# Second output group of a two-layer trunk in seven products, its fourth token sum in another buffer, large transfers in pieces

## The chip, the cores and the metric

The kernel runs on one core of one Trainium2 chip. The metric is the device time of one execution in microseconds; less is better. The engines are named as the profile names them: PE is TensorE's matmul, PEld its weight load, DVE is VectorE, ACT is ScalarE, POOL is GpSimd, SP is SyncE, which here only issues transfers.

## What is computed

Two layers over 1024 tokens of 2048 features, all in float32. Each layer is one large input projection (2048 to 4352), a small middle part, and one large output projection (2048 to 2048) that is added to x:

```python
for l in range(DEPTH):                                    # DEPTH = 2
    h = _rmsnorm(x, norm_gain[l])
    proj = jnp.einsum('bsd,de->bse', h, w_in[l])
    q, k, v, g_attn, x_rnn, g_rnn = jnp.split(proj, splits, axis=-1)
    attn = _swa_sink_attention(q, k, v, sinks[l], cos, sin)
    xc = _causal_conv(x_rnn, conv_w[l], conv_b[l])
    rnn = _rg_lru(xc, w_rgate[l], b_rgate[l], w_igate[l], b_igate[l], lru_param[l])
    mixed = jnp.concatenate([attn * jax.nn.silu(g_attn), rnn * jax.nn.silu(g_rnn)], axis=-1)
    x = x + jnp.einsum('bse,ed->bsd', mixed, w_out[l])
return _rmsnorm(x, final_gain)
```

`_rg_lru` has two gate matrices of 64x64 blocks on the convolved `xc`, then a scan over tokens.

## The kernel before

**Passes, groups, units.** The tokens are taken in two halves `h` of 512, the layers `l` in order, so there are four passes (h, l): (0,0), (0,1), (1,0), (1,1). In a pass the columns of both projections are cut into 25 groups of 256: groups 0 to 16 are the input projection, 17 to 24 the output projection (`PG = 17`). A plain group is 8 units; a unit is one 256 KB weight load and 12 matmuls of 512 tokens (three for each 128x128 block, since weights and operands are cut into a high and a low part, L719). Time inside a pass is counted in slots `s`, eight to a group; each engine's program runs through the same slots, in a fixed order within a slot, and engines meet only at semaphores.

**Seven products.** Groups in `SEVEN` (L68) take half of their inner dimension by a Strassen scheme over two halves of the features, the tokens and the columns: instead of four of the eight units they have seven units of 12 matmuls of 256 tokens (L740), four of them ("lead") in the slots of the group before. They need four weight sums S1 to S4, made ahead of time in DRAM, and four pairs of token sums. Before, these are the output groups 19 to 24 in every pass (23 as the last in (1,1)), and in (1,0) and (1,1) the input groups 7 to 15 too.

**Token sums of the output side.** `operand_sums` (four DVE instructions, L1381 to L1384) builds the raw sums of pair n in slot `T_AT[n]`; one slot later ACT cuts the high part (`xsum_cut_hi`, L950) and DVE the low part (`operand_sums_lo`, L1390). `T_ORDER` says which pair comes n-th. The buffers lie over storage that is free by then: pairs 0 and 1 over the end of `q`, 2 and 3 over the recurrent half of `mixed`, so that 2 and 3 wait until those tiles are cut.

**Weights.** SP issues the load of unit u+6 when unit u is done (`RING = 6`). In the slot of unit u, ACT cuts the high part of unit u+3 (`weight_hi`, L942) and DVE the low part (`weight_lo`, L1344; `AHEAD = 3`). From then on PE can run it.

**The recurrent tiles.** Eight tiles j start at slots `R0`. For the last, j = 7, that is slot 112: DVE does the convolution taps in slots 113 and 114 (L1604, L1607, L1609), cuts its low part into `xcut` in slot 116 (`conv_lo`, L1621), and PE runs the gate matmuls on it at the end of slot 117 (`gate`, L867), which wait for that cut (`xc_lo`) and stand in PE's one stream with everything else.

**Weight sums.** POOL makes them with transfers from DRAM to DRAM (copies L631, accumulating ones L637), in batches of up to two groups. `OPENS` holds the batches at which POOL waits for a later unit, so the batches run in stretches: 5, 6, 2 and 3 before.

**Other large transfers.** In (1,1) SP spills x in four transfers of 1 MB (slots 1 to 4); in (1,0) it stores the first half's output in four of 1 MB (slots 22, 30, 38, 46); in (0,1) it loads the next half's x in two bursts (slots 148 and 196). Where they stand in SP's queue they stand before the next weight load.

Of the kernel before, what the change touches and what calls it, by code (L numbers as in the profile page):

```python
# [13 lines left out]
P = 128  # L14
DEPTH = 2
D = 2048
SEQ = 1024
TOK = 512
# [49 lines left out]
SEVEN = {(h, l): (*IN_SEVEN[h, l], *range(PG + 2, PG + (7 if (h, l) == (LAST, DEPTH - 1) else 8)))  # L68
# [121 lines left out]
def tile_of(what, t):  # L190

    return 2 * GROUPS.index((what, t // 2)) + t % 2
# [35 lines left out]
OPENS = {5: (0, 1, 1), 11: (1, 0, 4), 13: (1, 1, 8)}  # L228
# [16 lines left out]
def build(nc, xt, w, blocks, gates, par, fgain, cossin, ident, out):  # L245
    with ExitStack() as ctx:
        def sb(name, shape, dt=F32):
            return ctx.enter_context(nc.sbuf_tensor(name, [P, *shape], dt))
# [23 lines left out]
        gt = sb("gt", [TOK])  # L272
        prob = sb("prob", [2, 2, 2, P])
# [23 lines left out]
        idn = probT[:, 0, 0, 0, :]  # L297
# [4 lines left out]
        t_at = {"out": [(q_end if i < 2 else mixed_end) - (2 - i % 2) * t_size for i in range(NPAIR)]}  # L302
# [190 lines left out]
        def _(sp_):  # L493
# [36 lines left out]
            for h in range(HALVES):  # L530
                for l in range(DEPTH):
                    for s in range(SLOTS):
# [18 lines left out]
                        if (h, l, "in") in ZONES and l == 1 and s - SPILL_AT in range(4):  # L551
                            i = SPILL[s - SPILL_AT]

                            sp_.wait_ge(evac, at_evac(h, 0, tile_of("o", 4 * i + 3)))
                            sp_.dma_start(x_kept[i], x[:, 4 * i:4 * i + 4, :].rearrange("p k t -> p (k t)")
                                          ).then_inc(kept[i], 16)
                        for i in range(KT // 2):
                            if (h, l) in X_BACK and s == RELOAD + 2 * i:

                                if (h, l, "in") in ZONES:  # L560
                                    sp_.wait_ge(unit_done, TURNED[h, l, "in"])
                                if l == 0:
                                    if h > 0:
                                        sp_.wait_ge(stored[i // 2], 16 * h)
                                    sp_.dma_start(x[:, 2 * i:2 * i + 2, :], xt[h, :, 2 * i:2 * i + 2, :]
                                                  ).then_inc(xres_in[i], 16)
                                else:
                                    sp_.wait_ge(kept[i // 2], 16 * sum(at < (h, l) for at in X_BACK if at[1] == 1) + 16)
                                    half = i % 2 * 2 * TOK
                                    sp_.dma_start(x[:, 2 * i:2 * i + 2, :].rearrange("p k t -> p (k t)"),  # L570
                                                  x_kept[i // 2, :, half:half + 2 * TOK]).then_inc(xres_in[i], 16)
                        for a, b in STORES_W:
                            if h > 0 and l == 0 and s == NS + 2 * b:

                                sp_.wait_ge(scaled, (h - 1) * KT + b)
                                sp_.dma_start(out[h - 1, :, a:b, :], x[:, a:b, :]).then_inc(stored[a // 4], 16)
# [6 lines left out]
                        if l == 1 and s == O0 + 12 and h == LAST:  # L583

                            sp_.wait_ge(v_done, per_layer(h, l, NP, NP))
                            sp_.dma_start(idn, ident).then_inc(idn_in, 16)
                        if l == 1 and s == O0 + 12 and h < LAST:

                            sp_.wait_ge(op_lo, at_op(h, 1, 1, KT - 1))
                            sp_.wait_ge(xsum_done, at_t(h, 1, "out", NPAIR - 1))  # L590
                            for i in range(KT // 4):
                                x_load(h + 1, i)
                        if l == 1 and s == O0 + (OG - 1) * UPG + 4 and h < LAST:

                            sp_.wait_ge(unit_done, TURNED[h, 1, "out"])
                            for i in range(KT // 4, KT // 2):
                                x_load(h + 1, i)
# [17 lines left out]
            for n in stored:  # L615
                sp_.wait_ge(n, 16 * LAST)
# [54 lines left out]
        def _(pe):  # L671
# [233 lines left out]
            def fin_transposes(n):  # L905
# [13 lines left out]
                for k in range(4):  # L919
                    t0 = HT + P * c  # L920
                    last = pe.transpose(fin_bank(n)[:, P * k:P * k + P], x[:, 4 * g + k, t0:t0 + P], idn[:, :])
# [14 lines left out]
        def _(act):  # L936
# [7 lines left out]
            def xsum_cut_hi(h, l, zone, n):  # L944
# [3 lines left out]
                if zone == "out" and i >= 2:  # L948
                    act.wait_ge(op_lo, at_op(h, l, 1, AT + RT // 2 * (i - 1) - 1))
# [373 lines left out]
        def _(dve):  # L1323
# [23 lines left out]
            def operand_sums(h, l, zone, n):  # L1347
# [6 lines left out]
                if zone == "in":  # L1354
# [3 lines left out]
                    if l == 1:  # L1358
                        dve.wait_ge(kept[T_ROOM[i]], 16 * sum(at <= (h, l) for at in X_BACK if at[1] == 1))
                        dve.wait_ge(op_lo, at_op(h, l, 0, KT - 1))  # L1360
                        dve.wait_ge(acc_done, at_acc(h, KT * 2))
                    else:
                        for k in (pair, pair + 1):
                            dve.wait_ge(x_sem(k), 16 * (h + 1))
                        if h > 0:
                            dve.wait_ge(stored[T_ROOM[i]], 16 * h)
# [12 lines left out]
                if i >= 2:  # L1379
                    dve.wait_ge(op_lo, at_op(h, l, 1, AT + RT // 2 * (i - 1) - 1))  # L1380
# [544 lines left out]
```

## Time and profile before

| | us |
|---|---|
| median of 3 runs | 2288.71 |
| lowest and highest | 2285.85, 2288.94 |
| the profiled execution's own time | 2291.39 |
| its span | 2289.6 |

| engine | busy us | share of the span |
|---|---|---|
| PE | 2278.3 | 100% |
| PEld | 1940.8 | 85% |
| DVE | 1567.5 | 68% |
| ACT | 1313.7 | 57% |
| POOL | 84.7 | 4% |

The mean granted clock of TensorE over the span is 0.999 of full speed. PE is never long idle, so what an edit is worth is read from PE's own rows (how far one matmul starts after the other, where a gap stands) and from the other engines' rows in the slots where PE waits for them. A shift of any other engine's work costs only what reaches PE.

### The profile page before, as it was taken

To read this page: it belongs to the slowest core of one execution; us is meant where nothing else is said; L and a number is where in the kernel's file an instruction comes from. 1 tells how busy PE (TensorE), PEld (TensorE's weight loads), DVE (VectorE), ACT (ScalarE), POOL (GpSimd) and SP (SyncE) were. 2 spreads that over 40 slices of the span, in tenths; PEclk is the share of its full clock that TensorE was granted. 3 is DMA by queue.
4 is the path that set the end of the run, shared out by engine and by line. 5 is a ranking of instruction groups with operands and counts; after the bars stand their busy time and mean duration, and the time that the engine had idled before them with its cause. 6 is when DMAs were issued, how large, how long until landed. Compare 5 with 4: busy or idle time off the path is not lost.

```text
span 2289.6 us, 38210 instructions
## 1 busy us (share of the span) xinstructions
PE 2278.3 (100%) x14446; PEld 1940.8 (85%) x14446; DVE 1567.5 (68%) x2594; ACT 1313.7 (57%) x2536; POOL 84.7 (4%) x138
## 2 busy tenths in 40 slices
PE   9999999999999999999999999999999999999998
PEld 7878888899888888889987888888988888888898
DVE  7658878656546876856677777686568468778555
ACT  6558666444445867645665576663446557566444
POOL 0110000000111000000010000000001100000000
PEclk9999999999999999999999999999999999999999
DMA  8988777544788877644476466664447746666444
GB/s 246 240 247 264 240 243 237 157 134 143 198 243 235 261 236 239 213 142 139 138 231 182 158 206 195 219 190 147 139 134 255 194 134 198 205 201 199 139 134 152
DMA packets 173271, 447.01 MB, mean 195 GB/s; under 512 B 20768, under 2 KB 25120, under 8 KB 167200
## 3 DMA queue, kind: packets, MB, share of 16 engines
q1 hardware_dynamic: 165744, 381.56, 52.3%
q0 software_dynamic: 6912, 62.92, 11.6%
q8 instruction: 114, 1.87, 0.3%
q14 instruction: 69, 0.57, 0.1%
q10 hardware_dynamic: 432, 0.10, 0.0%
HBM read 365.85 MB, written 141.56 MB: 222 GB/s over the span
## 4 chain that ended last, share of the span: by engine, by line
PE 95%; DMA 2%; DVE 2%; ACT 1%; issue 0%; POOL 0%; DVEq 0%; ACTq 0%; POOLq 0%
PE proj L719 71%; PE proj L740 18%; DMA wall<-in_w 2%; PE ps_at L848 2%; PE ps_at L823 1%; PE ps_at L867 1%; PE proj L759 1%; DMA wall<-in_blocks 0%; DVE wcut L1344 0%; ACT wcut L942 0%; ACT gy L1048 0%; PE proj L786 0%; PE ps_at L674 0%; DVE mixed L1828 0%; DVE rstd L1457 0%
## 5 line engine op out<-in xcount | busy, mean ns | idle before, releaser
L719 PE MATMUL proj<-operand,wcut 128*128 128x512 f32 x7512 | 1747.9, 391 | 3.5 <-DVE gy L1476 2.2
L719 PEld LDWEIGHTS proj<-operand,wcut 128*128 128x128 f32 x7512 | 1400.9, 188 | 302.6 <-issue 8.6
L1344 DVE TENSOR_TENSOR wcut<-wall,wcut 128x512 fp32r<-128x512 f32 x799 | 549.9, 688 | 548.0 <-ACT wcut L942 541.2
L942 ACT ACTIVATE wcut<-wall 128x512 fp32r<-128x512 f32 x798 | 501.7, 629 | 605.2 <-DMA wall<-in_w 326.4
L740 PEld LDWEIGHTS proj<-operand,wcut 128*128 128x128 f32 x1476 | 187.8, 191 | 6.5
L740 PE MATMUL proj<-operand,wcut 128*128 128x256 f32 x1476 | 189.8, 283 | 0.0
L740 PE MATMUL proj<-xsum_out,wcut 128*128 128x256 f32 x1104 | 136.8, 283 | 0.0
L740 PEld LDWEIGHTS proj<-xsum_out,wcut 128*128 128x128 f32 x1104 | 134.9, 192 | 0.6
L740 PE MATMUL proj<-xsum_in,wcut 128*128 128x256 f32 x864 | 111.8, 284 | 0.0
L740 PEld LDWEIGHTS proj<-xsum_in,wcut 128*128 128x128 f32 x864 | 107.9, 191 | 3.5 <-issue 1.7
L1048 ACT ACTIVATE gy<-proj 32x512 f32<-32x512 f32 x144 | 85.0, 590 | 15.5 <-PE proj L719 8.7
L1100 ACT ACTIVATE prob<-ps_at,stat 128x128 f32<-128x128 f32 x256 | 90.3, 367 | 0.7
L1139 ACT ACTIVATE sqr<-ps_at,pars 64x512 f32<-64x512 f32 x64 | 43.8, 685 | 59.0 <-PE ps_at L867 58.5
L1113 ACT ACTIVATE mixed<-ps_at 64x256 f32<-64x256 f32 x128 | 48.6, 380 | 42.6 <-PE ps_at L848 38.6
L1005 ACT ACTIVATE sqr<-x 128x512 f32<-128x512 f32 x62 | 37.0, 635 | 55.9 <-DVE x L1654 55.9
L1654 DVE TENSOR_TENSOR x<-proj,x 128x512 f32<-128x512 f32 x62 | 39.9, 686 | 39.7 <-PE proj L719 39.6
L631 POOL DMA_DIRECT2D weight_sums<-in_blocks x32 | 16.1, 511 | 1353.3 <-PE proj L719 1353.1
L1439 DVE TENSOR_TENSOR acc<-acc,sqr 128x512 f32<-128x512 f32 x80 | 55.2, 690 | 4.9 <-ACT sqr L1005 0.2
L637 POOL DMA_DIRECT2D weight_sums<-in_blocks x64 | 51.0, 861 | 178.9 <-DMA weight_sums<-weight_sums 97.1
L1100 ACT ACTIVATION_READ_ACCUMULATOR prob<-ps_at,stat 128x1 f32 x256 | 52.8, 206 | 0.0
L1539 DVE TENSOR_TENSOR gy<-proj,rstd 128x512 f32<-128x512 f32 x56 | 38.5, 687 | 18.9 <-PE proj L719 18.3
L1607 DVE SCALAR_TENSOR_TENSOR xc<-xr,pars,xc 128x512 f32<-128x512 f32 x64 | 47.9, 749 | 1.4
(186 smaller groups left out, 1734.2 us busy)
## 6 DMA issues: line engine op xcount, KB each, us to landing
wall<-in_w SPq DMA_DIRECT2D x494, 256.0 KB, 2.8
weight_cuts<-wcut SPq DMA_DIRECT2D x126, 512.0 KB, 4.0
wcut<-weight_cuts SPq DMA_DIRECT2D x126, 512.0 KB, 4.1
weight_sums<-in_blocks POOLq DMA_DIRECT2D x84, 512.0 KB, 6.5
wall<-weight_sums SPq DMA_DIRECT2D x164, 256.0 KB, 2.7
wall<-in_blocks SPq DMA_DIRECT2D x141, 256.0 KB, 2.8
weight_sums<-weight_sums POOLq DMA_DIRECT2D x28, 512.0 KB, 5.0
x<-in_xt SPq DMA_DIRECT2D x16, 512.0 KB, 3.7
```

What stands on the lines that cost most here:

```text
L637: pool.dma_start(sums[SUMS[to], l, g:g + size].rearrange("g r e -> (g r) e"), blocks[WHOLE[what], l, g:g + size].rearrange("g r e -> (g r) ...
L719: last = pe.matmul(bank_of(l, 2 * g + m)[:, :], wcut[:, n % RING, a, c:c + P], operand[:, k, b, :], start=(i == 0 and k == 0), stop=(k == ...
L740: last = pe.matmul(bank_of(l, 2 * g + m)[:, HT * half:HT * half + HT], wcut[:, n % RING, a, P * i:P * i + P], src, start=(kind == "lead" a ...
L848: last = pe.matmul(ps_v[HD * i:HD * i + HD, t, :, :], vkey[kv][rows, 2 * c + b, :], probT[rows, :, i, :, SB * b:SB * b + SB], start=b == 0 ...
L942: act.activation(wcut[:, u % RING, 0, :], wall[:, u % RING, 1, :], ACT.Copy).then_inc(w_hi, 1)
L1048: act.activation(gy[dst:dst + 32, 1, :], bank_of(l, tile)[src:src + 32, :], ACT.Copy).then_inc(shift_done, 1)
L1100: act.activation(prob[:, odd, i, pair, :], ps_s[:, odd, i, pair, :], ACT.Exp, scale=HD ** -0.5, bias=stat[:, 1, odd, i, pair:pair + 1], ac ...
L1113: act.activation(mixed[HD * odd:HD * odd + HD, TPK * kv:TPK * kv + TPK, t0:t0 + CH], ps_v[HD * i:HD * i + HD, :, odd, :], ACT.Copy).then_i ...
L1139: act.activation(r_in[a:a + HD, :], ps_at[a:a + HD, 3, :], ACT.Tanh, scale=0.5, bias=pars[a:a + HD, l, C_BR + j:C_BR + j + 1]).then_inc(r_ ...
L1344: dve.tensor_tensor(wcut[:, u % RING, 1, :], wall[:, u % RING, 1, :], wcut[:, u % RING, 0, :].bitcast(F32), ALU.subtract).then_inc(w_lo, 1)
L1439: ins = dve.tensor_tensor(acc[:, :], acc[:, :], sqr[:, k % 2, :], ALU.add)
L1607: mark(dve.scalar_tensor_tensor(xc[:, :], src, wc, xc[:, :], ALU.mult, ALU.add))
```

## The change

1. Group 18, the second output group, is done in seven products too, in all four passes.
2. Its leads stand in the slots of group 17, so the token sums are made earlier: slots 113, 115, 127 and 135 in place of 126, 128, 136 and 143. The third to be made is now pair 3, and its buffer lies over `prob` and `probT`, the attention probabilities; the identity that was kept in `probT` goes to `kboth`.
3. Weight sums for group 18 are added, so there are 18 batches in place of 16, in stretches of 5, 5, 1, 2, 1 and 4. The two stretches of one batch start at slot 128 of (0,1) and of (1,0).
4. The spill goes in eight transfers of 512 KB (slots 1 to 8), the output store in sixteen of 256 KB (every second slot from 16 to 46), the loads of the next half's x one by one in slots 148, 152, 156, 160 and 196 to 199.

```diff
-SEVEN = {(h, l): (*IN_SEVEN[h, l], *range(PG + 2, PG + (7 if (h, l) == (LAST, DEPTH - 1) else 8)))
+SEVEN = {(h, l): (*IN_SEVEN[h, l], *range(PG + 1, PG + (7 if (h, l) == (LAST, DEPTH - 1) else 8)))
...
-T_AT = {(h, l, "out"): (126, 128, 136, 143) for h in range(HALVES) for l in range(DEPTH)}
+T_AT = {(h, l, "out"): (113, 115, 127, 135) for h in range(HALVES) for l in range(DEPTH)}
...
-T_ORDER = {(h, l, "out"): (0, 1, 2, 3) for h in range(HALVES) for l in range(DEPTH)}
+T_ORDER = {(h, l, "out"): (0, 1, 3, 2) for h in range(HALVES) for l in range(DEPTH)}
...
-OPENS = {5: (0, 1, 1), 11: (1, 0, 4), 13: (1, 1, 8)}
+OPENS = {5: (0, 1, 1), 10: (0, 1, 128), 11: (1, 0, 4), 13: (1, 0, 128), 14: (1, 1, 9)}
...
-        t_at = {"out": [(q_end if i < 2 else mixed_end) - (2 - i % 2) * t_size for i in range(NPAIR)]}
+        t_at = {"out": [q_end - 2 * t_size, q_end - t_size, mixed_end - 2 * t_size, prob_at]}
...
-                        if (h, l, "in") in ZONES and l == 1 and s - SPILL_AT in range(4):
+                        if (h, l, "in") in ZONES and l == 1 and s - SPILL_AT in range(8):
...
-                        for a, b in STORES_W:
-                            if h > 0 and l == 0 and s == NS + 2 * b:
+                        for k in range(KT):
+                            if h > 0 and l == 0 and s == NS + 2 * k + 2:
...
-                if i >= 2:
-                    dve.wait_ge(op_lo, at_op(h, l, 1, AT + RT // 2 * (i - 1) - 1))
+                if i == 2:
+                    dve.wait_ge(op_lo, at_op(h, l, 1, AT + RT // 2 - 1))
+                if i == 3:
+                    dve.wait_ge(pt_done, per_layer(h, l, NP, NP))
```

The instructions of DVE in slots 115 and 116 of pass (0,0), up to the cut that the gate of tile 7 waits for (`xcut`). Lines above 620 are two to four higher in the changed kernel. Before:

```order
L1344 TENSOR_TENSOR wcut<-wall,wcut 128x512
L1637 SCALAR_TENSOR_TENSOR mu<-sqr,mu 128x512
L1614 TENSOR_TENSOR gwcut<-gw,gwcut 128x2x128
L1344 TENSOR_TENSOR wcut<-wall,wcut 128x512
L1621 TENSOR_TENSOR xcut<-xc,xcut 64x512 x2
```

And in the changed kernel:

```order
L1346 TENSOR_TENSOR wcut<-wall,wcut 128x512
L1385 TENSOR_TENSOR xraw_out_59<-mixed 128x256
L1386 TENSOR_TENSOR xraw_out_59<-mixed,xraw_out_59 128x256
L1387 TENSOR_TENSOR xraw_out_59<-mixed 128x256
L1388 TENSOR_TENSOR xraw_out_59<-mixed,xraw_out_59 128x256
L1641 SCALAR_TENSOR_TENSOR mu<-sqr,mu 128x512
L1618 TENSOR_TENSOR gwcut<-gw,gwcut 128x2x128
L1346 TENSOR_TENSOR wcut<-wall,wcut 128x512
L1394 TENSOR_TENSOR xsum_out_51<-xraw_out_59,xsum_out_51 128x1024
L1625 TENSOR_TENSOR xcut<-xc,xcut 64x512 x2
```

The sums of pair 1 and the cut of their low part now stand ahead of the cut for the gate. Those of pair 0 (xraw_out_58 and xsum_out_50) stand likewise in slots 113 and 114, just ahead of these rows.

PE in pass (0,0), from the last gate matmul of tile 7 to the first two leads. Before:

```order
L867 MATMUL ps_at<-xcut,gwcut 128x512 x2
L719 MATMUL proj<-operand,wcut 128x512 x348
L740 MATMUL proj<-operand,wcut 128x256 x12
L719 MATMUL proj<-operand,wcut 128x512 x12
L740 MATMUL proj<-xsum_out_50,wcut 128x256 x3
```

And in the changed kernel:

```order
L869 MATMUL ps_at<-xcut,gwcut 128x512 x2
L721 MATMUL proj<-operand,wcut 128x512 x252
L742 MATMUL proj<-operand,wcut 128x256 x12
L721 MATMUL proj<-operand,wcut 128x512 x12
L742 MATMUL proj<-xsum_out_50,wcut 128x256 x3
```

The first lead comes 96 matmuls, which is one plain group, earlier, and the pattern that follows it is one group longer.

## Rows read from the trace of the kernel before

**Rows 1.** The page, part 1: busy time, share, instructions of each engine.
```profile
PE 2278.3 (100%) x14446; PEld 1940.8 (85%) x14446; DVE 1567.5 (68%) x2594; ACT 1313.7 (57%) x2536; POOL 84.7 (4%) x138
```

**Rows 2.** The chain in order of time: start us, us, what; pass (0,0).
```profile
365.29 78.92 PE proj L719 x348
...
482.04 8.19 PE proj L719 x36
...
503.04 8.19 PE proj L719 x36
```

**Rows 3.** Timeline (start us, us, instruction, [idle before]) of (0,0), slots 113 to 119.
```profile
344.69 0.69 DVE L1344 TENSOR_TENSOR wcut<-wall,wcut 128x512 fp32r<-128x512 f32 x1 [1.84 <-ACT wcut L942]
...
354.40 1.40 DVE L1621 TENSOR_TENSOR xcut<-xc,xcut 64x512 fp32r<-64x512 f32 x2
...
358.72 0.62 PE L867 MATMUL ps_at<-xcut,gwcut 128*128 128x512 f32 x2
...
362.87 1.42 DVE L1344 TENSOR_TENSOR wcut<-wall,wcut 128x512 fp32r<-128x512 f32 x2 [2.17 <-ACT wcut L942]
```

**Rows 4.** Timeline of DVE where the token sums stand before, slots 126 to 128.
```profile
386.18 0.42 DVE L1381 TENSOR_TENSOR xraw_out<-mixed 128x256 f32<-128x256 f32 x1
...
387.90 0.68 DVE L1539 TENSOR_TENSOR gy<-proj,rstd 128x512 f32<-128x512 f32 x1
...
954.80 1.23 DVE L1390 TENSOR_TENSOR xsum_out<-xraw_out,xsum_out 128x1024 fp32r<-128x1024 f32 x1 [0.47 <-ACT xsum_out L950]
955.98 0.69 DVE L1344 TENSOR_TENSOR wcut<-wall,wcut 128x512 fp32r<-128x512 f32 x1
```

**Rows 5.** Who waited for L1621 (us, times), and the timeline of (0,1).
```profile
  PEld ps_at L867: 0.8, 2
...
925.13 1.40 DVE L1621 TENSOR_TENSOR xcut<-xc,xcut 64x512 fp32r<-64x512 f32 x2
...
929.45 0.62 PE L867 MATMUL ps_at<-xcut,gwcut 128*128 128x512 f32 x2
```

**Rows 6.** Timeline of (1,0), slots 114 to 117; last, the high cut.
```profile
1491.64 0.63 ACT L942 ACTIVATE wcut<-wall 128x512 fp32r<-128x512 f32 x1 [3.30 <-DMA wall<-weight_sums]
1492.38 0.69 DVE L1344 TENSOR_TENSOR wcut<-wall,wcut 128x512 fp32r<-128x512 f32 x1 [2.60 <-ACT wcut L942]
1493.10 0.75 DVE L1607 SCALAR_TENSOR_TENSOR xc<-xr,pars,xc 128x512 f32<-128x512 f32 x1
...
1498.87 1.41 DVE L1621 TENSOR_TENSOR xcut<-xc,xcut 64x512 fp32r<-64x512 f32 x2
...
1502.90 0.63 PE L867 MATMUL ps_at<-xcut,gwcut 128*128 128x512 f32 x2
...
1522.58 1.06 ACT L950 ACTIVATE xsum_out<-xraw_out 128x1024 fp32r<-128x1024 f32 x1 [3.67 <-DVE xraw_out L1384]
```

**Rows 7.** Timeline of (1,1), slots 114 to 117.
```profile
2052.34 0.63 ACT L942 ACTIVATE wcut<-wall 128x512 fp32r<-128x512 f32 x1 [2.38 <-DMA wall<-weight_sums]
...
2053.80 0.75 DVE L1607 SCALAR_TENSOR_TENSOR xc<-xr,pars,xc 128x512 f32<-128x512 f32 x1
...
2059.57 1.40 DVE L1621 TENSOR_TENSOR xcut<-xc,xcut 64x512 fp32r<-64x512 f32 x2
...
2064.51 0.63 PE L867 MATMUL ps_at<-xcut,gwcut 128*128 128x512 f32 x2
```

**Rows 8.** Around 1215 us: chain, PE's timeline, windows (stretch, busy times, PEclk, DMA).
```profile
1199.27 10.87 DMA wall<-in_w
...
1217.14 5.04 PE L719 MATMUL proj<-operand,wcut 128*128 128x512 f32 x14 [1.81 <-DVE gy L1476]
...
1217.40:1220.90 3.50, 3.50 (x10) 2.68 (x10) 3.34 (x7) 3.37 (x6) 0.00 (x0) 0.52 0.96 255
```

**Rows 9.** POOL's timeline there, and the page's weight loads (count, KB, us to landing).
```profile
1197.64 1.60 POOL L637 DMA_DIRECT2D weight_sums<-in_blocks  x2 [0.61 <-DMA weight_sums<-in_blocks]
...
wall<-in_w SPq DMA_DIRECT2D x494, 256.0 KB, 2.8
```

More of the change, by code:

```diff
@@ L272, in build @@
         gt = sb("gt", [TOK])
+        prob_at = nc.sbuf_base
         prob = sb("prob", [2, 2, 2, P])
@@ L567, in _ @@
                                 else:
-                                    sp_.wait_ge(kept[i // 2], 16 * sum(at < (h, l) for at in X_BACK if at[1] == 1) + 16)
+                                    sp_.wait_ge(kept[i // 2], 32 * sum(at < (h, l) for at in X_BACK if at[1] == 1) + 32)
                                     half = i % 2 * 2 * TOK
@@ L583, in _ @@
                         if l == 1 and s == O0 + 12 and h == LAST:
-                            sp_.wait_ge(v_done, per_layer(h, l, NP, NP))
+                            sp_.wait_ge(s_done, per_layer(h, l, NP, NP) + 1)
                             sp_.dma_start(idn, ident).then_inc(idn_in, 16)
[L587 to L591, printed above, removed]
+                        for i in range(KT // 4):
+                            if l == 1 and s == O0 + 12 + 4 * i and h < LAST:
+                                if i == 0:
+                                    sp_.wait_ge(op_lo, at_op(h, 1, 1, KT - 1))
+                                    sp_.wait_ge(xsum_done, at_t(h, 1, "out", NPAIR - 1))
                                 x_load(h + 1, i)
-                        if l == 1 and s == O0 + (OG - 1) * UPG + 4 and h < LAST:
-                            sp_.wait_ge(unit_done, TURNED[h, 1, "out"])
-                            for i in range(KT // 4, KT // 2):
+                        for i in range(KT // 4, KT // 2):
+                            if l == 1 and s == O0 + (OG - 1) * UPG + i and h < LAST:
+                                sp_.wait_ge(unit_done, TURNED[h, 1, "out"])
                                 x_load(h + 1, i)
@@ L615, in _ @@
             for n in stored:
[L616 removed]
+                sp_.wait_ge(n, 64 * LAST)
         @block.gpsimd
@@ L920, in fin_transposes @@
                     t0 = HT + P * c
-                    last = pe.transpose(fin_bank(n)[:, P * k:P * k + P], x[:, 4 * g + k, t0:t0 + P], idn[:, :])
+                    last = pe.transpose(fin_bank(n)[:, P * k:P * k + P], x[:, 4 * g + k, t0:t0 + P], idn)
                 last.then_inc(fin_t, 1)
@@ L947, in xsum_cut_hi @@
                 act.wait_ge(xsum_done, at_t(h, l, zone, n))
-                if zone == "out" and i >= 2:
-                    act.wait_ge(op_lo, at_op(h, l, 1, AT + RT // 2 * (i - 1) - 1))
+                if zone == "out" and i == 2:
+                    act.wait_ge(op_lo, at_op(h, l, 1, AT + RT // 2 - 1))
                 act.activation(xsum[zone][i][:, HI_PART[zone][i], :, :], xraw[zone][i][:, :, :],
@@ L1358, in operand_sums @@
                     if l == 1:
-                        dve.wait_ge(kept[T_ROOM[i]], 16 * sum(at <= (h, l) for at in X_BACK if at[1] == 1))
+                        dve.wait_ge(kept[T_ROOM[i]], 32 * sum(at <= (h, l) for at in X_BACK if at[1] == 1))
                         dve.wait_ge(op_lo, at_op(h, l, 0, KT - 1))
```

17 lines of the change are left out of this document (9 added, 8 removed).

## The prediction

> **What bounds the kernel now.** I read the page first. PE is busy for 2278.3 of 2289.6 us [rows 1], so there are two ways to change the time: change how long PE's own stream is, or change how long PE stands still in it. I then read the chain in order of time for the price of a group [rows 2], the timelines of DVE and PE at the slots into which work is moved [rows 3 to 7], and the largest standstill of PE that the trace has [rows 8, 9]. The reader is to see that DVE, busy 68% of the span on average, has no free time in the few slots that matter.
>
> The profiled execution took 2291.39 us, 2.7 above the median of 2288.71. I make the sum against 2291.4 and take the 2.7 off at the end.
>
> **Group 18 in seven products.** 348 plain matmuls take 78.92 us, so one starts 0.2268 us after the other, and a plain group of 96 takes 21.77 us [rows 2]. A group in the seven-product pattern repeats after 503.04 - 482.04 = 21.00 us [rows 2]; that holds 48 matmuls of 512 and 84 of 256 tokens. The pattern moves one group forward and becomes one group longer, so each pass saves 0.77 us, four passes **3.1 us**. It is all on PE, so all of it is on the path. The three additional weight units of each pass and the lead copies fall into slots 137 to 151. Nothing of that is new in kind: the groups behind it run the same work at the 21.00 us period without PE waiting. The pair sums that stood in slots 126 to 129 and at 143 leave this region, so DVE is less late there than before. I cost it at nothing; if a weight cut came late, it would cost its delay, some tenths.
>
> **The first two token sums, moved to slots 113 and 115.** This is the term that decides. The four raw sums of a pair take 387.90 - 386.18 = 1.72 us of DVE from the first to the next instruction, the low cut 955.98 - 954.80 = 1.18 us [rows 4], so a pair costs 2.90 us and two pairs 5.80 us. All of it now stands ahead of L1621, the cut on which the gate matmuls of tile 7 wait. DVE and ACT run their instructions in program order, so L1621 moves by what is put ahead of it, less the idle time that DVE has in between.
>
> Pass (0,0): DVE waits before the weight cut at 344.69 and not again until 362.87 [rows 3]. The sums stand behind the cut at 344.69, so nothing of the wait before it hides them. L1621 ends at 354.40 + 1.40 = 355.80; the gate starts at 358.72. The cover is 2.92 us, the shift 5.80, so PE stands still for **2.9 us**. I followed ACT through the same slots: its high cut of a pair takes 1.06 us [rows 6] and is ready before DVE comes to the low cut, so it adds nothing.
>
> Pass (0,1): L1621 ends at 926.53, the gate starts at 929.45 [rows 5]. The cover is again 2.92, the standstill **2.9 us**.
>
> Pass (1,0): here the raw sums of pair 0 fit into the 2.60 us in which DVE waits for a weight cut [rows 6]. ACT's cut of them can start behind its weight cut, at 1491.64 + 0.63 = 1492.27, and ends about 1493.35. DVE's low cut then ends about 1494.55, where L1607 started at 1493.10 before: a shift of 1.45. The sums of pair 1 and their low cut add 2.90, 4.35 in all. The cover is 1502.90 - 1500.28 = 2.62 [rows 6], the standstill **1.7 us**, some of it at the unit before the gate, whose weight cut is late as well.
>
> Pass (1,1): the same shape, with ACT's weight cut ending at 2052.97 and L1607 at 2053.80 [rows 7], so again a shift of 4.35. The cover is 2064.51 - 2060.97 = 3.54, the standstill **0.8 us**.
>
> Together 8.3 us. That PE does wait at this place is in the trace: tile 5 of (0,0) and of (0,1) has next to no cover and PE waited twice there, 0.8 us in all [rows 5]. The ends: 0, if I overlook cover; 11.2, if DVE's idle time in (1,0) and (1,1) hid nothing (5.80 - 2.62 and 5.80 - 3.54 in place of 1.7 and 0.8). A gain is excluded, since nothing is taken from DVE ahead of L1621. I take 8.3, as every part of it is a difference of two rows. Behind the standstill PE's other suppliers have that much more time, so nothing else is late next.
>
> **What a standstill does to the clock.** When PE had been idle for 1.81 us before 1217.14, the granted clock of the next 3.50 us was 0.52, that is the lower level, 1.2 GHz, for nearly all of it [rows 8]. That costs 3.50 x (1 - 0.52) = 1.7 us on top. The standstills in (0,0) and (0,1) are longer than that one, so I expect the same fall there: **3.4 us**. In (1,0) the 1.7 us come in two parts; in (1,1) they are short. The ends are 0 and 6.8, for no falls and four.
>
> The Trainium skill, "TensorE: Matmul & The Clock Gate", section "Why this matters for your kernels", bounds the idle gaps that keep full clock by a length that is greater than the one in rows 8. By that rule the falls would not come and the sum would be 3.4 us lower; the row disagrees, and I take the row. It stays as the second rival.
>
> **Transfers and the stretches of POOL.** Weight loads land in 2.8 us by the median [rows 9]; the one issued at 1199.27, while POOL had three accumulating transfers under way, took 10.87 us, and through ACT and DVE it led to the 1.81 us wait and the slow clock behind it, 3.5 us in all [rows 8, 9]. In the changed kernel the batch at that place is the one of a single group, so that two of the three transfers have half the size, and the first 1 MB store is in pieces. I expect most of the 3.5 us to go. Against it stand two new places: the single batch at slot 128 of (1,0), which runs beside the reload of x (8 transfers of 512 KB), and the fourth batch in (1,1). Each could cost from nothing to the 3.5 us of rows 8. The pieces of the spill and of the loads for the next half delay a weight load less than the whole ones did; PE waits for neither now, so they give nothing. The wait of DVE for the probabilities (`pt_done`) is met 20 slots before. For this whole part I take **-2.0 us**, between -3.5 (it goes, nothing new) and +3.5 (it stays or goes, one or two new ones).
>
> **The sum.** 2291.4 - 3.1 + 8.3 + 3.4 - 2.0 = 2298.0 against the profiled execution, and 2.7 less against the median: **2295** (+6.6 us, +0.29%). About 0.2%, or 4.6 us, is what a measurement of this kernel can tell from no change.
>
> **The rivals.**
> First, the sums are hidden after all: DVE reaches slot 113 earlier than I think, or the gate of tile 7 has more cover. Then -3.1 - 2.0 remain and the time is 2283.6, at the edge of faster. For it: DVE is idle 2.17 us just behind these slots [rows 3], and in (1,0) 2.60 us within them. Against it: the rows of (0,0) and (0,1) show no idle time between the sums' place and L1621, and the order puts them ahead of it. It decides from a shift of under 2.92 us, half of what I find. Chance 0.12.
> Second, PE waits as worked out but keeps 2.4 GHz: 2295.3 - 3.4 = 2291.9, within 0.2%. For it: the fall is seen once in this trace; against it: the gap there was shorter. Chance 0.22.
> Third, the new places of POOL's batches cost more: the wait at 1215 us stays and one more like it comes, +3.5 in place of -2.0, which gives 2300.8. For it: 10.87 us for a 2.8 us load [rows 8, 9]; against it: POOL's 16 batches bring PE one long wait in this whole trace. Chance 0.13.
> Fourth, the change doesn't do what it says: PE comes to the second lead of group 18 before the last sum is cut (slots 135 and 136 for a use in slot 141), and the 3.1 us are lost in waiting: 2298.4. Against it: before, the distance was about the same (143 and 144 for 149). Chance 0.05.
>
> **How the numbers follow.** The forecast, gate waits with the fall of the clock in at least one pass, has the remaining 0.48. Slower by over 0.2% (above 2293.3): most of the forecast (0.42), the third and the fourth, 0.60. Faster by over 0.2% (below 2284.1): some two thirds of the first, 0.08. Within: the second, the rest of the first and of the forecast, 0.32. The range goes from 2289.0, under the second rival with its waits a third smaller, to 2300.5, into the third; outside lie the first and half of the third, 0.19.
>
> **What would show it.** Four waits of PE at the gate matmuls (L869) for DVE's `xcut` (L1625), of 2.9, 2.9, 1.7 and 0.8 us, near 361, 931, 1500 and 2060 us, and nowhere else new; a granted clock near 0.5 for some 3.5 us behind the first two; the 21.00 us period one group earlier in each pass; no idle PE near 1215 us, or less. It is wrong if PE waits at none of the four gates, if it waits with the clock at full speed, or if a weight load of over 10 us in slots 128 to 142 of (1,0) or in slots 20 to 50 of (1,1) ends in a wait of PE.

## The result, and the profile of the changed kernel

The changed kernel takes 2295.79 us (median of 7, 2293.10 to 2298.67), the kernel before on the same chip 2288.44 us (median of 7, 2285.85 to 2289.28). The ratio is 1.0032, 95% interval 1.0022 to 1.0042: slower by 0.32%. 2295 was forecast.

The profiled execution took 2298.67 us, the slowest of the seven, with a span of 2296.9 us and a mean granted clock of 0.998. The page's line on the engines and the line on the weight loads (count, KB, us to landing):

```profile
PE 2278.2 (99%) x14590; PEld 1945.4 (85%) x14590; DVE 1582.5 (69%) x2622; ACT 1323.1 (58%) x2556; POOL 95.0 (4%) x154
...
wall<-in_w SPq DMA_DIRECT2D x478, 256.0 KB, 3.0
```

PE's waits (for whom, us in total, times, longest):

```profile
PE ps_at L869 <- DVE xcut L1625: 7.0, 4, 2.8
PE ps_at L869 <- ACT sqr L1143: 1.3, 2, 1.1
```

L869 and L1625 are L867 and L1621 of before. PE's busy time is the same as in [rows 1], with 144 matmuls more, and the span is 7.3 us longer: the first place to look is a wait, and there is one line of 7.0 us that before didn't have. The timeline of the gate of tile 7 in the four passes (start us, us, instruction, [idle before]), with the DVE rows ahead of the first, answers [rows 3, 5 to 7]:

```profile
355.96 0.43 DVE L1385 TENSOR_TENSOR xraw_out<-mixed 128x256 f32<-128x256 f32 x1
...
359.34 1.23 DVE L1394 TENSOR_TENSOR xsum_out<-xraw_out,xsum_out 128x1024 fp32r<-128x1024 f32 x1
360.60 1.40 DVE L1625 TENSOR_TENSOR xcut<-xc,xcut 64x512 fp32r<-64x512 f32 x2
...
362.06 0.95 PE L869 MATMUL ps_at<-xcut,gwcut 128*128 128x512 f32 x2 [2.81 <-DVE xcut L1625]
...
935.55 0.99 PE L869 MATMUL ps_at<-xcut,gwcut 128*128 128x512 f32 x2 [2.81 <-DVE xcut L1625]
...
1507.88 0.73 PE L869 MATMUL ps_at<-xcut,gwcut 128*128 128x512 f32 x2 [0.99 <-DVE xcut L1625]
...
2071.63 0.73 PE L869 MATMUL ps_at<-xcut,gwcut 128*128 128x512 f32 x2 [0.43 <-DVE xcut L1625]
```

In each pass the gate starts 0.06 us after L1625 ends, where before it started 2.6 to 3.5 us after. The windows behind the four waits, and the stretch in which [rows 8] had its wait (stretch, its length, busy times, PEclk, DMA share, GB/s):

```profile
362.06:365.50 3.44, 3.44 (x9) 2.74 (x10) 3.34 (x5) 2.39 (x3) 0.00 (x0) 0.55 0.29 116
935.55:939.00 3.45, 3.45 (x9) 2.71 (x10) 3.35 (x5) 2.35 (x3) 0.00 (x0) 0.54 0.38 153
1507.90:1511.00 3.10, 3.10 (x19) 2.84 (x20) 3.03 (x5) 2.67 (x4) 0.00 (x0) 1.00 0.79 278
2071.60:2075.00 3.40, 3.37 (x20) 3.04 (x21) 3.33 (x5) 2.28 (x3) 0.00 (x0) 1.00 0.85 275
...
1205.00:1225.00 20.00, 20.00 (x90) 16.55 (x89) 16.33 (x28) 15.12 (x25) 2.57 (x4) 1.00 0.85 226
```

Behind the two long waits PE runs at 1.2 GHz (9 matmuls in 3.44 us), behind the two short ones at 2.4. Near 1215 us PE no longer waits. The chain shows the period of a group in seven products, one group earlier than in [rows 2]:

```profile
444.32 8.19 PE proj L721 x36
...
465.32 8.19 PE proj L721 x36
```

If PE's timeline is cut at the starts of slots (the first matmul of each), the difference of the two profiled executions falls into these stretches:

| pass, slots | before | after | difference |
|---|---|---|---|
| (0,0), 104 to 120 | 46.91 | 51.58 | +4.67 |
| (0,1), 112 to 136 | 66.33 | 70.99 | +4.66 |
| (1,0), 112 to 136 | 59.12 | 60.24 | +1.12 |
| (1,1), 112 to 136 | 58.91 | 59.59 | +0.68 |
| all four, 136 to 176 (groups 17 to 21) | 4 x 112.32 | 3 x 111.56 + 111.75 | -2.85 |
| (1,0), 0 to 64 (the wait near 1215 us) | 193.54 | 189.73 | -3.81 |
| (0,1), 0 to 64 | 185.65 | 184.50 | -1.15 |
| (1,0) and (1,1), 64 to 112 | 287.28 | 290.05 | +2.77 |
| everything else | | | +1.2 |

The sum is +7.3. Of the +2.77, 1.9 us are idle time of PE at three other gates, where it waits for ACT (the second line of waits above, and one of 0.5 us); the rest is matmuls that start later around these waits. The longest, 1.1 us near 2053 us, came when ACT had waited 4.78 us for the load of a weight sum. The runs below show waits of this kind at changing places, so they are no part of the explanation.

### The profile page after: what moved, and what is told of

It reads as the page before. It is cut to its first block, busy times and chain, and to the rows that moved or that the text cites. A ratio compares the mean times of both kernels' runs of the same rounds, so it can differ in the third digit from the quotient of the medians.

```text
span 2296.9 us, 38643 instructions
## 1 busy us (share of the span) xinstructions
PE 2278.2 (99%) x14590; PEld 1945.4 (85%) x14590; DVE 1582.5 (69%) x2622; ACT 1323.1 (58%) x2556; POOL 95.0 (4%) x154
## 4 chain that ended last, share of the span: by engine, by line
PE 92%; DVE 3%; DMA 2%; ACT 1%; issue 1%; SPq 0%; DVEq 0%; ACTq 0%
PE proj L721 69%; PE proj L742 19%; PE ps_at L850 2%; PE ps_at L825 1%; PE ps_at L869 1%; DMA wall<-in_w 1%; DMA wall<-weight_sums 1%; DVE wcut L1346 1%; PE proj L761 1%; ACT wcut L944 0%; DVE xcut L1625 0%; DVE xsum_out L1394 0%; PE proj L788 0%; DVE xc L1611 0%; ACT L1141 0%
## 5 line engine op out<-in xcount | busy, mean ns | idle before, releaser
L721 PE MATMUL proj<-operand,wcut 128*128 128x512 f32 x7320 | 1706.6, 391 | 0.9 <-DVE wcut L1346 0.5
L721 PEld LDWEIGHTS proj<-operand,wcut 128*128 128x128 f32 x7320 | 1365.5, 188 | 291.9 <-issue 9.2
L1346 DVE TENSOR_TENSOR wcut<-wall,wcut 128x512 fp32r<-128x512 f32 x811 | 558.6, 689 | 549.5 <-ACT wcut L944 542.9
L944 ACT ACTIVATE wcut<-wall 128x512 fp32r<-128x512 f32 x810 | 509.2, 629 | 596.8 <-DMA wall<-in_w 312.5
L742 PEld LDWEIGHTS proj<-operand,wcut 128*128 128x128 f32 x1620 | 206.1, 191 | 7.2
L742 PE MATMUL proj<-operand,wcut 128*128 128x256 f32 x1620 | 208.3, 283 | 0.0
L742 PE MATMUL proj<-xsum_out,wcut 128*128 128x256 f32 x1296 | 160.5, 283 | 0.0
L742 PEld LDWEIGHTS proj<-xsum_out,wcut 128*128 128x128 f32 x1296 | 158.2, 192 | 0.6
L633 POOL DMA_DIRECT2D weight_sums<-in_blocks x36 | 18.2, 512 | 1356.3 <-PE proj L721 1355.9
L639 POOL DMA_DIRECT2D weight_sums<-in_blocks x72 | 57.5, 858 | 195.9 <-DMA weight_sums<-weight_sums 106.9
L869 PE MATMUL ps_at<-xcut,gwcut 128*128 128x512 f32 x128 | 41.4, 405 | 8.9 <-DVE xcut L1625 7.0
```

What stands on the lines that cost most here:

```text
L639: pool.dma_start(sums[SUMS[to], l, g:g + size].rearrange("g r e -> (g r) e"), blocks[WHOLE[what], l, g:g + size].rearrange("g r e -> (g r) ...
L721: last = pe.matmul(bank_of(l, 2 * g + m)[:, :], wcut[:, n % RING, a, c:c + P], operand[:, k, b, :], start=(i == 0 and k == 0), stop=(k == ...
L742: last = pe.matmul(bank_of(l, 2 * g + m)[:, HT * half:HT * half + HT], wcut[:, n % RING, a, P * i:P * i + P], src, start=(kind == "lead" a ...
L869: last = pe.matmul(ps_g, gwcut[:, part, a, :], xcut[:, part, :], start=a == 0, stop=a == 1)
L944: act.activation(wcut[:, u % RING, 0, :], wall[:, u % RING, 1, :], ACT.Copy).then_inc(w_hi, 1)
L1346: dve.tensor_tensor(wcut[:, u % RING, 1, :], wall[:, u % RING, 1, :], wcut[:, u % RING, 0, :].bitcast(F32), ALU.subtract).then_inc(w_lo, 1)
```

## The experiments

The theory: the loss is the wait at the gate of tile 7, set by the DVE work that now stands ahead of L1625, plus the slow clock behind the two long waits; the seven products and the transfers give time back. The rivals: the gate waits cost nothing or leave the clock alone; the loss, or the gain, lies in the transfers and POOL's batches. Each kernel ran beside the kernel before, whose median was 2288.14 us beside e1 to e4, 2287.94 beside e5 to e8 and 2287.64 beside e9 to e12 (27 to 33 runs each). These three groups ran on three chips, so between groups the ratios are the safer comparison.

| run | median us | runs | ratio to before, 95% interval |
|---|---|---|---|
| e1, sums behind the gate's cut | 2283.57 | 11 | 0.9977 (0.9968 to 0.9985) |
| e2, early sums alone | 2300.99 | 5 | 1.0055 (1.0042 to 1.0067) |
| e3, one pair ahead | 2284.75 | 11 | 0.9984 (0.9975 to 0.9993) |
| e4, a pair and a half | 2288.50 | 11 | 1.0001 (0.9993 to 1.0010) |
| e12, 0.43 us more | 2290.61 | 11 | 1.0016 (1.0007 to 1.0025) |
| e5, whole transfers | 2286.64 | 11 | 0.9997 (0.9988 to 1.0005) |
| e10, loads single, others whole | 2283.70 | 11 | 0.9982 (0.9973 to 0.9991) |
| e7, before with pieces | 2287.26 | 11 | 1.0003 (0.9994 to 1.0012) |
| e6, old stretches | 2293.92 | 6 | 1.0030 (1.0018 to 1.0042) |
| e11, one batch joined | 2283.82 | 11 | 0.9982 (0.9973 to 0.9991) |
| e8, group 18 plain, old stretches | 2289.22 | 11 | 1.0009 (1.0000 to 1.0018) |
| e9, group 18 plain, its sums made | 2284.94 | 11 | 0.9989 (0.9981 to 0.9998) |

**e1: the sums behind the cut.** The changed kernel with one line different:

```diff
-T_AT = {(h, l, "out"): (113, 115, 127, 135) for h in range(HALVES) for l in range(DEPTH)}
+T_AT = {(h, l, "out"): (118, 120, 127, 135) for h in range(HALVES) for l in range(DEPTH)}
```

> The changed kernel, with the sums of pairs 0 and 1 in slots 118 and 120, that is behind the cut that the gate of tile 7 waits for, in place of 113 and 115. All else stays as changed. Theory (gate waits and the fall of the clock behind them): the four waits of PE at the gate, 2.81 + 2.81 + 0.99 + 0.43 = 7.0 us in the trace of the changed kernel, go, and the two stretches of 3.4 us at a clock of 0.5 go with them, 2 x 1.7 = 3.4 us: 2295.8 - 7.0 - 3.4 = 2285.4. Rival 1 (PE waits, but the slow clock costs nothing that is not made up): 2288.8. Rival 2 (the time comes from the new transfer places, POOL's batches or the pieces, and the gate waits are made up elsewhere): 2295.8 stays.

2283.57 us, 12.2 less than the changed kernel (11.9 when each is measured from the kernel before beside it) and below the kernel before. PE waits at no gate for `xcut` any more, L1625 ends 2.7 to 3.9 us ahead of the gates, and the clock stays up (window of e1, at the place of the first fall):

```profile
358.50:362.00 3.50, 3.50 (x16) 2.83 (x16) 3.33 (x7) 2.69 (x4) 0.00 (x0) 1.00 0.93 339
```

So two numbers in a table cost the changed kernel all that it loses. 12.2 is nearer to the 10.4 expected than to the rivals' 7.0 and 0; both rivals fall.

**e2: the early sums alone**, in the kernel before:

```diff
-T_AT = {(h, l, "out"): (126, 128, 136, 143) for h in range(HALVES) for l in range(DEPTH)}
+T_AT = {(h, l, "out"): (113, 115, 136, 143) for h in range(HALVES) for l in range(DEPTH)}
```

> The kernel before, with only the sums of pairs 0 and 1 moved to slots 113 and 115; group 18 stays plain, the transfers stay whole, the batches stay in their stretches. Theory: this one edit brings the whole loss, 2288.4 + 7.0 (four gate waits) + 3.4 (two falls of the clock) = 2298.8, with the four waits at the gate of tile 7 and the clock near 0.5 behind the first two. Rival 1 (waits without a cost of the clock): 2295.4. Rival 2 (transfers, or the seven products of group 18, are what costs): 2288.4, no change.

2300.99 us, +12.9. PE's waits for `xcut` come back (five; the fifth, 1.67 us, is at another tile's gate near 186 us), and the clock behind the first two gates falls again. Waits of PE in e2:

```profile
PE ps_at L867 <- DVE xcut L1621: 9.3, 5, 2.8
```

And its windows behind the two gates (PEclk is the third number from the end):

```profile
361.00:364.50 3.50, 3.48 (x11) 2.78 (x12) 3.40 (x5) 2.65 (x4) 0.00 (x0) 0.68 0.27 107
935.50:939.00 3.50, 3.45 (x8) 2.71 (x9) 3.37 (x5) 2.27 (x4) 0.00 (x0) 0.53 0.25 99
```

The same edit costs the same with none of the rest of the change present: e1 and e2 show the cause from both sides. That +12.9 is above the 10.4 is in part pass (1,0), whose slots 112 to 136 grew by 3.12 us, since PE also waited 1.04 and 0.51 us at two units ahead of the gate.

**e3, e4 and e12: how much work ahead of the cut costs.** All three are the changed kernel with other slots for pairs 0 and 1: `(113, 120, ...)` in e3, `(113, 116, ...)` in e4, and in e12 that of e4 with one sum repeated:

```diff
-                mark(dve.tensor_tensor(to[0], first[:, 0:HT], first[:, HT:TOK], ALU.subtract))
+                for _ in range(2 if n == 1 else 1):
+                    mark(dve.tensor_tensor(to[0], first[:, 0:HT], first[:, HT:TOK], ALU.subtract))
```

> The changed kernel with pair 0 in slot 113 and pair 1 in slot 120: only one pair stands ahead of the gate's cut. Theory (the cut has a cover of 2.92 us in (0,0) and (0,1), and only what exceeds it costs): a shift of 2.90 us just fits, so no gate wait over 0.1 us and no fall of the clock: 2285.4, like the run with both pairs behind. Rival (each pair ahead of the cut costs its share, cover or not): half of the 10.4 us stays, 2290.6.

2284.75 us. One pair is 2.90 us, the cover 2.92, and it does fit: the gates of (0,0) and (0,1) start 0.06 us behind L1625 with no idle time in the row. The rival, half the loss, falls. The rows of (0,1) in e3:

```profile
924.21 1.40 DVE L1625 TENSOR_TENSOR xcut<-xc,xcut 64x512 fp32r<-64x512 f32 x2
...
925.67 0.72 PE L869 MATMUL ps_at<-xcut,gwcut 128*128 128x512 f32 x2
```

> The changed kernel with pair 0 in slot 113 and pair 1 in slot 116: the raw sums of pair 1 still stand ahead of the gate's cut, their low cut stands behind it. The shift is 2.90 + 1.72 = 4.62 us. Theory: waits of 4.62 - 2.92 = 1.7 us in (0,0) and (0,1), 1.45 + 1.72 - 2.62 = 0.55 in (1,0), none in (1,1): 3.95 us. If waits of 1.7 us bring the clock down as the 1.81 us before 1217 us did, 3.4 us more: 2285.4 + 3.95 + 3.4 = 2292.8. Rival (a wait of 1.7 us at this place leaves the clock at full speed): 2289.4. Rival 2 (the loss has nothing to do with the gate): 2295.8.

2288.50 us, 4.9 above e1 where waits of 3.95 were expected. Waits of PE in e4:

```profile
PE ps_at L869 <- DVE xcut L1625: 4.3, 3, 1.7
```

And the windows over and behind the first, and behind the second:

```profile
358.20:361.70 3.50, 1.82 (x8) 1.34 (x8) 3.37 (x6) 2.54 (x4) 0.00 (x0) 1.00 0.89 327
361.70:365.00 3.30, 3.30 (x16) 2.71 (x15) 3.23 (x4) 3.13 (x5) 0.00 (x0) 1.00 0.12 43
...
932.50:936.00 3.50, 3.50 (x18) 2.88 (x17) 3.43 (x4) 3.09 (x5) 0.00 (x0) 1.00 0.22 41
```

The waits came out as worked out, 1.7 us in (0,0) and (0,1); the clock did not fall. The 0.55 us expected in (1,0) did not come: L1625 ended 0.31 us ahead of that gate. The third wait of the line, 0.97 us, is at another tile's gate, near 161 us; waits of that kind at 160 to 190 us also stand in e2 and e5.

> The run with a pair and a half ahead of the gate's cut (2288.5 us), with the first of the four raw sums of the second pair done twice, which puts 0.43 us more ahead of the cut. Theory (each us that is put ahead of the cut is a us of wait at all four gates, since no cover is left): waits of 1.68 + 0.43 = 2.1 us in (0,0) and (0,1), some 0.5 in (1,0), 1.0 in (1,1), together 1.5 us longer: 2290.0, if a wait of 2.1 us leaves the clock at full speed as those of 1.68 us did. If it brings the clock down as those of 2.81 us did, 3.4 us more: 2293.4. Rival (the wait is not set by DVE's order): 2288.5.

2290.61 us, 2.1 above e4 (3.4 by the two ratios), between the two expected values. The trace says why: two equal waits of 2.1 us (waits of PE in e12, where L1626 is L1625),

```profile
PE ps_at L869 <- DVE xcut L1626: 4.3, 2, 2.1
```

the first followed by full clock, the second by a fall (windows of e12):

```profile
362.00:365.50 3.50, 3.50 (x17) 2.88 (x17) 3.43 (x5) 2.40 (x4) 0.00 (x0) 1.00 0.38 114
...
932.00:935.60 3.60, 3.60 (x11) 2.82 (x10) 3.53 (x5) 3.51 (x5) 0.00 (x0) 0.56 0.07 28
```

These two waits give the price of a fall without any subtraction of a wait: slots 104 to 120 of (0,0), at full clock, are 2.36 us longer than before, and slots 112 to 136 of (0,1), with the fall, 4.02, so the fall costs 1.66. The waits expected in (1,0) and (1,1), 0.5 and 1.0 us, were 0 and 0.08. The 11 runs of e12 spread over 2287.69 to 2293.00 us, with mean clocks from 1.000 (the fastest) to 0.998 (three of the five slowest); none to two falls of 1.7 us would fit that, but only the one run was profiled.

**e5, e7 and e10: the pieces.** e5 is e1 with whole transfers and bursts, e10 is e5 with the loads of the next half's x one by one again, e7 is the kernel before with the pieces and the new buffer alone. The edit that tells e5 from e10:

```diff
-                        for i in range(KT // 4):
-                            if l == 1 and s == O0 + 12 + 4 * i and h < LAST:
-                                if i == 0:
+                        if l == 1 and s == O0 + 12 and h < LAST:
...
+                            for i in range(KT // 4):
                                 x_load(h + 1, i)
```

> The kernel with the sums behind the gate's cut (2283.6 us), with the spill and the output store in four transfers of 1 MB each and the loads of the next half's x in two bursts, as before. Theory (PE waits for none of these transfers, nor for a weight load that stands behind them): 2283.6, within 1 us. Rival (a whole transfer ahead of a weight load delays it until PE waits, as near 1217 us before, and the clock falls): up to 3.5 us more, 2287.1, with a wait of PE for a weight cut near 1200 to 1240 us or in the first slots of (1,1).

2286.64 us, 3.1 above e1 (4.6 by the two ratios): the theory, and the step of the prediction that it repeats, falls. The chain of it in e5, behind slot 152 of (0,1): SP issues the burst, then weight loads; ACT waits for one of them, DVE for ACT, PE for DVE:

```profile
1020.95 1.37 SPq L501 DMA_DIRECT2D mixed<-in_xt  x3
1022.37 2.12 SPq L516 DMA_DIRECT2D wall<-in_w  x3
...
1029.69 1.37 ACT L943 ACTIVATE wcut<-wall 128x512 fp32r<-128x512 f32 x2 [5.43 <-DMA wall<-in_w]
...
1030.43 0.69 DVE L1345 TENSOR_TENSOR wcut<-wall,wcut 128x512 fp32r<-128x512 f32 x1 [6.05 <-ACT wcut L943]
...
1031.27 2.99 PE L720 MATMUL proj<-operand,wcut 128*128 128x512 f32 x12 [1.74 <-DVE wcut L1345]
```

The profile places 1.98 us of the 3.1 here: slots 136 to 176 of (0,1) take 113.54 us in e5 and 111.56 in e1.

> The kernel with the sums behind the gate's cut, with the spill and the output store whole (1 MB each), but the loads of the next half's x one by one. Theory (with group 18 in seven products the burst of loads in slot 148 of (0,1) is the one that PE waits for, 1.74 us near 1029 us in the run with whole transfers): the 3.1 us of that run go, 2283.6. Rival (the 1 MB spill or store costs them, by weight loads behind them): 2286.6 stays, with a wait of PE near 1200 to 1300 us or in the first slots of (1,1).

2283.70 us, level with e1 and 2.9 below e5 (3.4 by the two ratios): of the three kinds of pieces, it is the loads, and the whole spill and store cost nothing.

> The kernel before with the transfers in pieces and the fourth sum's buffer in the probabilities' place, and nothing else: group 18 plain, the sums in their old slots, the old stretches. Theory (nothing waits for the whole transfers, and the batch near 1200 us is what delays the load): no change against the kernel before, 2288.1. Rival (the 1 MB store is what delays the load near 1200 us): the wait near 1217 us and its slow clock go, 2284.6.

2287.26 us, no change. The same burst stands in the kernel before, and there the weight cuts behind it were done 0.74 and 0.33 us ahead of PE. With group 18 plain, slots 149 to 151 are 12.5 us of PE's work; in seven products they are 7.1 (2.88 + 1.44 + 2.75). So the loads need to be single only because group 18 is in seven products. A wait near 1213 us was there in e7's profile too, 1.0 us, with the clock at full speed behind it: the smaller pieces of the store are not what removes it. The loads there agree: the longest weight load issued between 1190 and 1240 us took 10.87 us before, 10.09 in e7 and 7.11 in the changed kernel, which has the smaller batch as well. A load that long is not always a wait of PE: one of 9.66 us in e6 cost nothing there.

**e6 and e11: the stretches.** Both are e1 with another line of `OPENS`:

```diff
-OPENS = {5: (0, 1, 1), 10: (0, 1, 128), 11: (1, 0, 4), 13: (1, 0, 128), 14: (1, 1, 9)}
+OPENS = {5: (0, 1, 1), 12: (1, 0, 4), 14: (1, 1, 8)}
```

for e6, and for e11 only the entry 13 is taken out.

> The kernel with the sums behind the gate's cut (2283.6 us), with POOL's 18 batches in stretches of 5, 7, 2 and 4, near those of the kernel before, in place of 5, 5, 1, 2, 1 and 4. Theory (the forecast's: the batch that ran near 1200 us beside the output store delayed a weight load to 10.87 us, and the new stretches put a smaller batch there): a load of about 10 us and a wait of PE of some 1.8 us come back near 1215 us, with the fall of the clock 3.5 us in a run that has them: 2285.5 to 2287.1. Rival (the pieces of the store alone took the wait away, or it comes and goes by itself): 2283.6.

2293.92 us, 10.4 above e1 (12.1 by the two ratios), in all six runs (2292.89 to 2295.53): far outside both theories, and not near 1215 us at all. The second stretch has one batch more and lasts until 794 us, where before it ended at 759 us. PE's and ACT's rows there, from the timeline of e6:

```profile
768.78 0.63 ACT L944 ACTIVATE wcut<-wall 128x512 fp32r<-128x512 f32 x1 [6.12 <-DMA wall<-in_blocks]
...
770.19 3.01 PE L721 MATMUL proj<-operand,wcut 128*128 128x512 f32 x12 [1.85 <-DVE wcut L1346]
779.32 2.01 PE L850 MATMUL ps_at<-probT,mixed 32*64 32x128 f32 x64 [6.12 <-ACT prob L1102]
```

The DMA view of e6 for 740 to 775 us (tile, count, KB, median us to landing):

```profile
weight_cuts<-wcut SPq DMA_DIRECT2D x7, 512.0 KB, 9.3
...
wall<-in_blocks SPq DMA_DIRECT2D x4, 256.0 KB, 8.9
```

In groups 7 to 15 of (0,1) SP also stores 512 KB weight cuts. With POOL's accumulating transfers beside them the four weight loads of the last row took 8.9 us by the median, where all 153 of that kind in e6 take 2.8. ACT waited for two of them, 6.12 us ahead of the weight cut at 768.78 and 1.96 ahead of the one at 772.08, and came to the attention behind them, `prob`, only at 774.97; so PE waited 6.12 us for `prob`, after which the clock was at 0.50. Before, the last batch ran beside such stores until 759 us and PE was busy throughout (25.00 of 25.00 us from 735 to 760): it is the part beyond that costs. Whether the stores are needed for it was not tested.

> The kernel with the sums behind the gate's cut, with the one batch of slot 128 of (1,0) joined to the two that start in slot 4 of (1,0); the one in slot 128 of (0,1) stays. Theory (only the batch that would run into slots 60 to 70 of (0,1) costs the 10.4 us of the run with the old stretches; a third batch in (1,0) runs while PE has plain groups and the weight cuts are read back): 2283.6 to 2287.1, the upper end if the wait near 1215 us comes. Rival (this batch is as dear as the other, by the output store beside it): 2290 or more, with a wait of PE between 1225 and 1260 us.

2283.82 us, level with e1. It is the batch in slot 128 of (0,1) that must be apart; the one in slot 128 of (1,0) costs nothing there and gives nothing.

**e8 and e9: the price of seven products.** e8 is e1 with group 18 plain, 16 batches and the old stretches; e9 keeps the 18 batches and new stretches, so that POOL makes weight sums which nothing reads:

```diff
-SEVEN = {(h, l): (*IN_SEVEN[h, l], *range(PG + 1, PG + (7 if (h, l) == (LAST, DEPTH - 1) else 8)))
+SEVEN = {(h, l): (*IN_SEVEN[h, l], *range(PG + 2, PG + (7 if (h, l) == (LAST, DEPTH - 1) else 8)))
...
-BUILT = [sorted({g for h in range(HALVES) for g in SEVEN[h, l]}) for l in range(DEPTH)]
+BUILT = [sorted({g for h in range(HALVES) for g in (*SEVEN[h, l], PG + 1)}) for l in range(DEPTH)]
```

> The kernel with the sums behind the gate's cut (2283.6 us), with group 18 plain again, so that there are 16 batches in the old stretches of 5, 6, 2 and 3. It differs from the run with the pieces alone only in where the four sums stand. Theory (seven products are worth 0.77 us a pass, 3.1 us in all, and the old stretches 0 to 3.5): 2286.7 without the wait near 1215 us, 2290.2 with it, and level with the run of the pieces alone. Rival (the seven products of group 18 give nothing, the gain lies in the transfers): 2283.6.

2289.22 us, a little above e7 though only the places and the order of the sums differ; its runs spread over 2285.39 to 2292.90 us. It says nothing exact on group 18. e9, with the new stretches of 18 batches, is 4.3 us less by the medians. Where these lie is not shown: e8's profiled run has no wait near 1215 us, and nearly all of its 2.2 us over e9's profiled run stands in (0,0) ahead of slot 104 (313.63 against 311.34).

> The kernel with the sums behind the gate's cut (2283.6 us), with group 18 plain, but with its weight sums still made by POOL in the same 18 batches and stretches (nothing reads them). It differs from the run with the sums later only in the work of PE and its suppliers for group 18, so the difference is the price of the seven products alone. Theory: 4 x 0.77 = 3.1 us longer, 2286.7. Rival 1 (the seven products give nothing): 2283.6. Rival 2 (the earlier run with group 18 plain, 2289.2, was longer because of the seven products and not of the old stretches): 2289.2.

2284.94 us, 1.4 above e1 by the medians, 0.12% or 2.7 us by the two ratios; above e10 and e11, which ran beside it, it is 1.2 and 1.1 by the medians and 1.6 by the ratios. In the traces slots 136 to 176 take 112.32 us in each pass of e9 and 111.56 in each of e1, 0.76 us a pass and 3.04 in all, without a wait of PE in either. PE's busy time differs by 1.6 us. The page of e9:

```profile
PE 2275.4 (100%) x14446; PEld 1940.0 (85%) x14446; DVE 1567.1 (69%) x2594; ACT 1312.6 (57%) x2536; POOL 95.0 (4%) x154
```

And that of e1:

```profile
PE 2273.8 (100%) x14590; PEld 1943.8 (85%) x14590; DVE 1582.6 (69%) x2622; ACT 1322.6 (58%) x2556; POOL 95.2 (4%) x154
```

The 3.04 us in the stream are shown. The runs suggest that some of it is lost again elsewhere, though the intervals (each about 2 us to a side) do not settle it, and the traces point the same way: slots 64 to 136 of (1,0) and (1,1) together take 406.0 to 408.1 us in the six profiles with group 18 in seven products and no wait at the gate of tile 7 (e1, e3, e5, e6, e10, e11), and 405.1 to 405.9 in the four with it plain (before, e7, e8, e9), 1.2 us more on the average. Part of it is gates that wait for ACT (0.8 us near 2040 us in e11); why was not tested. Two single profiles cannot be compared to a us: (0,0) ahead of slot 104 alone takes from 311.0 to 313.8 us in the fourteen, 313.1 in e1 and 311.3 in e9, for a reason that was not looked for.

## Why the prediction was right, point by point

**The bound** was named rightly: in (0,0) and (0,1) DVE has no free time in the slots that matter, and a shift of its work by more than the cover is a wait of PE, microsecond for microsecond. Against 2.92 us of cover, shifts of 2.90 (e3), 4.62 (e4), 5.05 (e12) and 5.80 us gave waits of 0, 1.68, 2.14 and 2.81. One reading that was given in support was wrong: the 0.8 us at tile 5 of (0,0) and (0,1) are in a row of PEld. There the weight load waited, and PE's rows at the same places have no idle time, so in the profile before no gate of a tile makes PE wait for `xcut`; the changed kernel's is the first to show it.

**Group 18**, -3.1: 4 x 0.76 = 3.04 in the stream (e1 against e9); in the changed kernel's own profile -2.85, with one short wait in (1,0). "It is all on PE, so all of it is on the path" is true of the stream; between whole kernels 1.1 to 2.7 us are left (e9 against e1, e10 and e11).

**The gate waits**, 8.3. Measured from slot to slot less the clock's share they are 2.97, 2.96, 1.12 and 0.68, 7.7 in all (7.0 as idle time in the rows). The first two, worked out of [rows 3 to 5], are right within 0.1 us. In (1,0) the shift was right: from the weight cut ahead of the sums to the end of L1625 it is 12.37 us (1495.45 to 1507.82) where it was 7.90 [rows 6], 4.47 us more against 4.35 forecast. The cover was mis-sized: that weight cut stood 10.5 us ahead of the gate before, and 11.4 in this run, because it waits for a load that lands a little earlier or later. Cover that begins at a load's landing is not a constant.

**The clock**, 3.4: 1.7 for each of two falls (1.66 in e12, where it can be read by itself), and none in (1,0) and (1,1), as forecast. By the rule of the Trainium skill that the prediction weighed (TensorE: Matmul & The Clock Gate, Why this matters for your kernels) the 2.81 us gaps would have kept full clock; here they did not, in either pass of the changed kernel or of e2, so the second rival falls at this wait. At waits of 1.7 us (e4) it would have been right.

**Transfers and stretches**, -2.0. The place that the term was made for gave more in the profile, -3.81 near 1215 us, though part of what it replaces comes and goes: the kernels with the old stretches show that wait at 1.81, 1.64 and 1.0 us and, in e8's profile, not at all. The third rival is out: the slots of the batch beside the reload are 0.19 us longer than in e1, and the one in (1,1) cost nothing. Against the medians the term lies between two measures: e1 less the seven products in the stream, 2283.57 - 2288.14 + 3.04 = -1.5, and e9 itself, which has everything but them, 2284.94 - 2287.64 = -2.7.

**What failed is a reason inside that term.** "PE waits for neither now, so they give nothing" priced the single loads in the kernel before, where it is true (e7). In the changed kernel, which has 5.4 us less of PE's work between the burst and the units behind it, whole bursts would have cost some 3 us (2.9, e5 less e10). The same holds for the stretches: they were priced by a wait of the kernel before, and not by where a batch more in the second stretch would have run, which is 10.4 us (e6). Both were in the changed kernel already, so the sum did not suffer; a reader who had left them out on the strength of this working would have lost some 13 us, if the two add up.

**The rest.** The first rival (sums hidden, 2283.6) is not what happened, but it is what e1 is: 2283.57. That the two agree to 0.03 us is luck, since the kernel before was 0.6 us lower beside e1 than in the forecast: from there, the terms other than the gate and the clock were forecast at -5.1 and came to -4.6, and the gate and the clock at 11.7 and came to 11.9. So the terms were right together, and the total is not a sum of large errors that cancel. The fourth rival is out; group 18's leads wait for nothing.

The version that beats both kernels is the change with the first two sums in slots 118 and 120, five slots later: 0.9977 of the time before, against 1.0032 for the change as it was made.

## What to carry to other kernels

When work is moved up on an engine that runs its program in order, as DVE did in these traces, find the first cut that another engine waits for behind its new place, and compare the work put ahead of it with the time between the end of that cut and its use: below it is free, beyond it costs its excess, and an excess of 2.8 us cost the clock as well each time here. Price each part of a change in the schedule that the whole change leaves, since a shorter stretch of the bounding engine takes cover away from transfers that were hidden before. Where a background batch is added, look up what else is in the queues at the place where the series now ends.

## What the runs showed of the hardware that was not expected

Equal waits do not have equal effects on the clock. Behind waits of 2.8 us it fell four times in four (the changed kernel and e2), behind two of 2.14 us once (e12), behind one of 1.81 us [rows 8]; it stayed at 2.4 GHz behind 1.85 (e6), 1.74 (e5), twice 1.68 (e4), and 1.67 and 1.64 us (e2, near 186 and 1225 us). The length of the wait alone does not decide it between 1.81 and 2.14 us; what does was not tested.

A 256 KB load took three times its usual time with no transfer of over 512 KB beside it: 8.9 us against a median of 2.8 when POOL's accumulating transfers and SP's stores of weight cuts ran side by side (e6, DMA engines 0.97 busy from 760 to 795 us).
